# A fused two-block transformer kernel on one core: the modulation and compression weights begun by a program on GpSimd instead of ScalarE, and the engines' loops written out

## The reference

```python
def first_block(x, c, ...):            # 2 layers
    for i in range(2):
        mod = silu(c) @ ada_w[i] + ada_b[i]            # 1024 x 6144: six vectors of 1024
        sh_a, sc_a, g_a, sh_f, sc_f, g_f = split(mod, 6)
        h = rms_norm(x, attn_norm[i]) * (1 + sc_a) + sh_a
        y = sparse_mixer(...) if i == 0 else diff_mixer(...)
        x = x + g_a * y
        h = rms_norm(x, ffn_norm[i]) * (1 + sc_f) + sh_f
        x = x + g_f * swiglu(h, gate[i], up[i], down[i])
    return x

def second_block(x, c, ctx, c_ctx, ...):   # 2 layers; 6 vectors each for x and for ctx
    # layer 0: pooling mixer and squared-ReLU MLP, on x and on ctx
    # layer 1: attention of x over ctx and x, and squared-ReLU MLP, on x
    return rms_norm(x, final_g)
```

## Time and profile before

| | us |
|---|---|
| median of 3 runs | 1786.71 (1785.96 to 1787.14) |
| span of the profiled execution | 1788.7 |
| PE busy in it | 1598.4 (89%) |
| DVE busy | 923.8 (52%) |
| ACT busy | 730.1 (41%) |
| POOL busy | 0.2 (0%) |

### The profile page before, as it was taken

One profiled execution on the slowest core, in us unless ns is written; L12 is line 12 of the kernel. 1 busy time (PEld: TensorE's weight loads), 2 busy tenths in 40 slices (PEclk: granted clock), 3 DMA queues, 4 the chain that ended last, 5 costly groups with the idle time before them and its releaser, 6 DMA issues.

```text
span 1788.7 us, 26203 instructions
## 1 busy us (share of the span) xinstructions
PE 1598.4 (89%) x10441; PEld 1347.2 (75%) x10441; DVE 923.8 (52%) x1534; ACT 730.1 (41%) x1064; POOL 0.2 (0%) x4
## 2 busy tenths in 40 slices
PE   3966998999989888999988999889999796989997
PEld 2753587899877656898767998678987673779985
DVE  2582245434566685433466445653355586354455
ACT  1431153433444433444334554344444443345543
POOL 0000000000000000000000000000000000000000
PEclk9987797999999889999998999889999897999998
DMA  9843702895545445998752645639756353536552
GB/s 354 303 136 123 249 29 71 279 306 170 185 135 173 143 163 167 308 306 301 266 191 71 187 165 190 199 101 307 251 188 204 102 183 97 165 121 188 165 190 80
DMA packets 165526, 335.94 MB, mean 188 GB/s; under 512 B 8128, under 2 KB 109128, under 8 KB 165192
## 3 DMA queue, kind: packets, MB, share of 16 engines
q1 hardware_dynamic: 134432, 226.71, 38.2%
q10 hardware_dynamic: 31016, 108.16, 18.2%
HBM read 333.79 MB, written 1.05 MB: 187 GB/s over the span
## 4 chain that ended last, share of the span: by engine, by line
PE 81%; DVE 12%; ACT 3%; DMA 2%; issue 2%; ACTq 0%; SPq 0%; DVEq 0%
PE ps L1526 21%; PE ps L1527 21%; PE ps L1528 21%; PE ps L1498 5%; PE ps L1667 2%; DVE wlo L930 2%; PE ps L1664 1%; DVE work L1015 1%; DVE res L1017 1%; PE ps L1752 1%; PE ps L1702 1%; PE ps L1735 1%; DMA ring<-in_ada_w_dram 1%; PE ps L1823 1%; PE ps L1731 1%
## 5 line engine op out<-in xcount | busy, mean ns | idle before, releaser
L930 DVE TENSOR_TENSOR wlo<-wraw,whi 128x1024 fp32r<-128x1024 f32 (+1 forms) x424 | 498.0, 1216 | 420.6 <-ACT whi L542 420.3
L542 ACT ACTIVATE whi<-wraw 128x1024 fp32r<-128x1024 f32 (+1 forms) x424 | 422.8, 1044 | 442.1 <-PE ps L1528 419.5
L1526 PE MATMUL ps<-hT_hi,whi 128*128 128x256 f32 x1472 | 422.6, 287 | 4.3 <-DVE hT_lo L1070 4.3
L1527 PE MATMUL ps<-hT_lo,whi 128*128 128x256 f32 x1472 | 417.0, 283 | 0.0
L1528 PE MATMUL ps<-hT_hi,wlo 128*128 128x256 f32 x1472 | 416.8, 283 | 0.0
L1526 PEld LDWEIGHTS ps<-hT_hi,whi 128*128 128x128 f32 x1472 | 282.4, 192 | 23.6 <-issue 23.4
L1528 PEld LDWEIGHTS ps<-hT_hi,wlo 128*128 128x128 f32 x1472 | 282.6, 192 | 0.0
L1527 PEld LDWEIGHTS ps<-hT_lo,whi 128*128 128x128 f32 x1472 | 282.5, 192 | 0.0
L1526 PE MATMUL ps<-whi,act_hi 128*128 128x512 f32 x560 | 219.3, 392 | 0.0
L1527 PE MATMUL ps<-wlo,act_hi 128*128 128x512 f32 x560 | 218.3, 390 | 0.0
L1528 PE MATMUL ps<-whi,act_lo 128*128 128x512 f32 x560 | 218.2, 390 | 0.0
(11 more groups left out here) (199 smaller groups left out, 1435.8 us busy)
## 6 DMA issues: line engine op xcount, KB each, us to landing
wraw<-in_mlp_w_dram SPq DMA_DIRECT2D x96, 1024.0 KB, 5.3
ring<-in_ada_w_dram ACTq DMA_DIRECT2D x90, 1024.0 KB, 5.2
wraw<-in_ffn_w_gate_dram SPq DMA_DIRECT2D x22, 1024.0 KB, 6.0
wraw<-in_ffn_w_up_dram SPq DMA_DIRECT2D x22, 1024.0 KB, 6.7
wraw<-in_ffn_w_down_dram SPq DMA_DIRECT2D x22, 1024.0 KB, 5.0
wraw<-in_diff_w_in_dram SPq DMA_DIRECT2D x12, 1024.0 KB, 5.0
wraw<-in_attn_w_qkv_dram SPq DMA_DIRECT2D x12, 1024.0 KB, 4.9
wraw<-in_sp_w_in_dram SPq DMA_DIRECT2D x8, 1024.0 KB, 12.7
```

Source lines behind the costliest of these rows:

```text
L542: nc.scalar.activation(whi[:, u % 2, part], wraw[:, u % 4, part], ACT.Copy).then_inc(hi_ready, 1)
L930: nc.vector.tensor_tensor(wlo[:, u % 2, part], wraw[:, u % 4, part], whi[:, u % 2, part].bitcast(F32), ALU.subtract).then_inc(lo_ready, 1)
L1526: mm(dst, s_hi, m_hi, start=start, stop=False, skip_group_check=skip)
L1527: mm(dst, s_hi, m_lo, start=False, stop=False, skip_group_check=skip)
```

## The change

All ring transfers are begun by a program of POOL that does nothing else. It runs through the units in order; the waits in `ring_dma` are the same. ACT's calls of `ring_fill`, `ada_step` and `ada_body_unit` are gone, with nothing in their place. A compression unit is now begun as two transfers of half the size, and PE waits for both. ACT keeps the bias transfers and those of the pooling matrices.

```diff
-        def ring_dma(eng, r, k=None):
+        def ring_dma(eng, r):
...
             if r >= EARLY.stop:
                 before = r - 1 - (len(EARLY) if r < EARLY.stop + 2 else 0)
-                eng.wait_ge(ring_used, before if k is None else k * 4 + before)
+                eng.wait_ge(ring_used, before)
...
                 dst = dst.rearrange("p (k e) -> p k e", k=8)
                 src = w1c[a][:, b * 8:(b + 1) * 8, :]
+                eng.dma_start(dst[:, 0:4, :], src[:, 0:4, :]).then_inc(sem("cmp_half"), 16)
+                dst, src = dst[:, 4:8, :], src[:, 4:8, :]
             eng.dma_start(dst, src).then_inc(early_full[r] if r in EARLY else ring_full[r % 2], 16)
...
+            if ring_unit(r)[0] == "cmp":
+                eng.wait_ge(sem("cmp_half"), 16 * (r - CMP_AT + 1))
...
-            ring_fill(1)
-            act.wait_ge(sem("small_params"), 128)
-            ring_fill(8)
             act.wait_ge(sem("modrow_zero"), 1)
             bias(0)
             act.wait_ge(sem("paramT_ready"), 1)
...
             norm_rows()
-            ada_step(8)
             split_unit(0)
...
             c0 = CMP_AT
-            ring_fill(c0 + 4)
             act.wait_ge(ring_used, c0 + 4)
...
             ins.then_inc(sem("cmp_silu"), 1)
-            ring_fill(c0 + 6)
-            ada_step(4)
             act.wait_ge(sem("cmp_shift"), 1)
             nc.scalar.activation(cmp_s, cmp_s, ACT.Exp, scale=float(HD) ** -0.5).then_inc(sem("cmp_exp"), 1)
-            ada_step(4)
...
+        @block.gpsimd
+        def _(pool):
+            ring_dma(pool, 0)
+            pool.wait_ge(sem("small_params"), 128)
+            for r in range(1, RING_UNITS):
+                ring_dma(pool, r)
```

The second part concerns the loops. In SP, ACT, DVE and PE each `Fori` over bodies of four units becomes a Python loop that writes out every unit, with constants instead of registers in waits and addresses. The order of the units is kept. On PE:

```diff
-                n = bodies(s_)
-                for first, many, ada in loops_of(name):
-                    if ada:
-                        bank7_wait()
-                    with pe.Fori(first, first + many) as k4:
-                        for j in range(4):
-                            hidden_unit(s_, j, k4)
-                            if ada:
-                                vector_unit(LOOP_PLAN[name][0], j, k4)
-                for i in range(4 * n, s_["count"]):
+                first, many = STREAM_PLAN.get(name, (0, 0))
+                for i in range(s_["count"]):
                     hidden_unit(s_, i)
+                    if i < 4 * many:
+                        vector_unit(first + i // 4, i % 4)
```

More of the change, by code:

```diff
@@ L504, in link @@
                 act.wait_ge(chain, chained[0])
[L506 to L521, removed]
             def bias(l):
@@ L574, in stream @@
                     act.wait_ge(hid_done, hid_base[name[4:]] + s_["count"])
-                n = bodies(s_)
-                for first, many, ada in loops_of(name):
-                    if ada and many == 1:
-                        for j in range(4):
-                            if s_["kind"] != "down":
-                                hidden_out(s_, j)
-                            split_unit(s_["base"] + j + 2)
-                            ring_fill(ring_at(LOOP_PLAN[name][0], j) + 3)
-                        continue
-                    with act.Fori(first, first + many) as k4:
-                        for j in range(4):
-                            split_weights(s_, j + 2, k4)
-                            if s_["kind"] != "down":
-                                hidden_out(s_, j, k4)
-                            if ada:
-                                ada_body_unit(name, j, k4)
-                    if ada:
-                        ring_next[0] += 4 * many
-                for i in range(4 * n, s_["count"]):
+                for i in range(s_["count"]):
+                    if i < s_["count"] - 2:
+                        split_unit(s_["base"] + i + 2)
                     if s_["kind"] != "down":
                         hidden_out(s_, i)
-                    if not (hold_last and i == s_["count"] - 1):
+                    if i == s_["count"] - 2 or i == s_["count"] - 1 and not hold_last:
                         split_unit(s_["base"] + i + 2)
@@ L811, in _ @@
             out_turn(1)
-            row_segment("out1", ada=True)
+            row_segment("out1")
             next_panel()
@@ L1621, in down_segment, with unit @@
                     mm(ps[:, D_BANKS[q], :], zero16[0:1, 0:P], zero16[0:1, :], start=True, stop=False, skip_group_check=True)
-                def unit(i, k4=None):
+                def unit(i):
                     u = s_["base"] + i
-                    last = k4 is None and i == s_["count"] - 1
+                    last = i == s_["count"] - 1
                     for kk, t in TILE_LAST if last else PAIR_LAST:
                         if t == 0:
-                            unit_wait(u, kk, k4)
+                            unit_wait(u, kk)
                         for h in range(2):
@@ L1636, in unit @@
                     ins.then_inc(unit_done, 1)
-                n = bodies(s_)
-                for first, many, ada in loops_of(name):
-                    if ada:
-                        for j in range(4):
-                            unit(j)
-                            vector_unit(LOOP_PLAN[name][0], j)
-                        continue
-                    with pe.Fori(first, first + many) as k4:
-                        for j in range(4):
-                            unit(j, k4)
-                for i in range(4 * n, s_["count"]):
+                first, many = STREAM_PLAN.get(name, (0, 0))
+                for i in range(s_["count"]):
                     unit(i)
+                    if i < 4 * many:
+                        vector_unit(first + i // 4, i % 4)
             def norm():
```

172 lines of the change are left out of this document (67 added, 105 removed).

## The result

| | before | after |
|---|---|---|
| median of 9 runs | 1787.14 us (1785.96 to 1791.89) | 1799.05 us (1793.69 to 1809.5) |
| profiled execution: time, span | span 1788.7 us | 1806.62, span 1804.8 us |
| granted clock of PE, mean | 0.934 | 0.928 |

The ratio is 1.0072, 95% interval [1.0048, 1.0095]: slower, by 0.7%. Forecast were 1785.0 us and a range up to 1795. The times of the changed kernel form two groups: five between 1793.7 and 1799.0 us, and four between 1805.0 and 1809.5 us. Its profiled execution is one of the upper group, and a part of its 16 us belongs to that group alone, as will be seen. The two groups differ in TensorE's clock: its mean over the run is 0.927 or 0.928 in the four upper ones and 0.933 to 0.936 in the five lower ones.

A forecast was written before the change was run, and what follows sets the result against it. The prediction took PE, busy 89% of the span, as the bound, with only its waits to win. Start -3.0 and compression stage +1.3 gave -1.7, taking the median 1786.71 to 1785.0 us; range 1778 to 1795.

The forecast's parts named there:

- The start, -3.0: Kernel start: ACT, freed of ring issues, begins the squares at about 14.2 instead of 17.20, gaining 3.0 us.
- the term for the tile's landing: Kernel start: the first weight tile still takes 9.09 us, sharing the bus with two ring transfers as before.
- A modulation unit by POOL, extra 1.0: Ring: from freed slot to landed data, a modulation unit begun by POOL takes 1.0 us more than by ACT.
- A compression unit by POOL, extra 2.0: Compression stage: a compression unit begun by POOL in two halves takes 2.0 us more than by ACT.
- the fourth lands later too, but behind 5.1 us of PE's work: Compression stage: 5.1 us of PE's work covers the fourth compression unit's later landing; PE is through at 170.9, not 168.9.
- +1.3 at its end: Compression stage: with extras of 1.0 and 2.0, the seventh modulation unit lands at about 201.3 against 199.97, costing 1.3 us.
- 1.0 extra is just hidden: Second attention: slack of 0.6 and some 0.3 us hides 1.0 us extra; beyond it each us costs one, once.
- The loops, 0: Written-out loops on all engines: PE has nothing to win, and fetching the longer program is costed at 0.
- stalls of a longer program: Whole kernel: stalls from the longer written-out program, given 0.04 of the chance of being slower by over 0.2%.
- the fourth rival: Kernel start: the earlier norm meets a full bus and gains nothing; only +1.3 is left, 1788 us; chance 0.12.
- the slow one: POOL's transfers take 2 to 3.5 us more each, compression waits grow; 1792 to about 1797 us; chance 0.27.
- The rival of the clock: Compression stage: PE's clock stays at 2.4 GHz and the stage ends some 6 us earlier; -9, 1778 us; chance 0.11.

The follow-up runs named there:

- e2: The kernel before with all loops of the four engines written out, ring still begun by ACT; 1786.5 us, ratio 0.9973.
- e12: The changed kernel, unaltered, profiled once more in a single run; 1793.65 us.
- e7: The changed kernel plus 52 filler products on PE in the pause near 600 us, ahead of the second attention; 1792.38 us, ratio 1.0011.
- e3: The changed kernel with the four compression units begun undivided by ACT, modulation units still by POOL; 1786.22 us, ratio 0.997.
- e4: The changed kernel with dynamic_dma_scratch_size 2048 instead of 1024 and a semaphore per compression unit for its halves; 1786.48 us, ratio 0.9986.
- e8: e3 plus 52 filler products on PE in the pause near 600 us, ahead of the second attention; 1781.58 us, ratio 0.9951.

## Why the prediction was wrong

- **What bounds the kernel**: right. The streams are PE's alone, and what moved lies at the start, in the compression stage and in the clock.
- **The start, -3.0**: the order of the steps was right and the size was not. The squares came 2.1 us earlier, the forecast had 3.0; the term for the tile's landing (9.09 kept) measured 9.90. Of seven profiles with ACT's ring the mean drift at 50 us is 0.0, of seven with POOL's -1.2: the start is worth about 1.2 us. The profiles with ACT's ring alone spread from -1.5 to +1.1, so a single one can't tell it, and by an estimate from that spread the gain is uncertain by some 0.4 us.
- **A modulation unit by POOL, extra 1.0**: right. In the chain above a freed slot (186.29) is followed by 0.44 until POOL begins and 5.85 to the landing, together 6.29, against 5.32; at 199.13 it is 0.30 + 5.58 against 5.18. That is 0.7 to 1.0. The landing alone gives 0.3 to 0.5 of it (median 5.7 against 5.2, or 5.4 with ACT's ring in e2), and the 0.3 to 0.44 until POOL begins come on top.
- **A compression unit by POOL, extra 2.0, and "the fourth lands later too, but behind 5.1 us of PE's work"**: this is the step that failed. I priced each transfer by itself and took it that two halves would be on their way together, as with ACT. The runs showed that with this setting POOL doesn't begin a half before the last one has landed: four halves take 18.5 us from the first issue (153.98) to the last landing (172.47). PE starts the third unit at 163.09, 1.0 later than forecast, but the fourth at 172.60, where the forecast's steps have it at 167.2. PE is through with the units at 177.9 instead of the 170.9 of my steps. The line with `dynamic_dma_scratch_size=1024` stood in the kernel's setup, and the trace of before had no transfer begun by POOL (its page lists no software queue) that could have shown its effect.
- **The rest of the compression stage, "+1.3 at its end"**: measured +6.4 and +4.7 in the two profiles against the first of before. PE's waits for the ring were forecast at about 4, 3, 1 to 2, 1 and 3 us, 12 to 13 in all; they came to 19.7, of which 10.4 at the compression units, where 4 had been forecast. Part of the 9 us comes back, since POOL begins the first modulation unit at 168.69, as early as ACT did, and it lands while PE is still with the compression units.
- **The second attention**: "1.0 extra is just hidden", right: PE doesn't wait for the ring there. Its clock was no step of my sum. I had the clock only as a gain of one stage; that a stretch of 24 us in another could come at half the clock (0.50), for 12 us, was in none of the rivals, and it makes the upper group and a part of the median.
- **The loops, 0**: right for the streams, to 0.01 us; the 2 to 4 us of the medians are open, as said above. The chances held 0.04 for stalls of a longer program and a little of the fourth rival. The profiles show no such stall, neither a place nor a price of one: PE's idle time with no releaser is 5.0 and 0.6 us in e2, as in the kernel before.
- **The rivals**: the slow one (0.27) has the sign and about the time (1792 to 1797), but by a mechanism that isn't the one found. It priced a slower transfer of every kind, deciding from 1.4 us of extra. The extra of the common kind stayed at 1.0, and it was only the order of the halves. Its top of about 1797 was near the lower group (median 1795.5); the range ended at 1795 and so missed the median of all nine runs, 1799.05. The rival of the clock (0.11) came out in part only: from 182 to 197 us the clock was 0.66 instead of 0.50, with PE idle for 3 us of the 15, and the stage ended later all the same.

In sum: the halves cost 9 to 11 us (by the drift of the compression stage, +5.7 in the mean of after, e12 and e7 and -3.2 in the mean of e3, e4 and e8, of which e7 has +6.0 and e8 -4.1; by the medians of e7 and e8, 10.8). The start gives about 1.2, and the modulation units by POOL together with it no difference that e2 and e3 can tell (0.3 us). The profiles put the rest at places where the clock changes.

## What to carry to other kernels

Before transfers are moved to GpSimd, look at how many of them must be on their way at once, and at `dynamic_dma_scratch_size` in the program's setup: here two halves of a unit began 0.75 us apart with 2048 and 4.6 to 4.7 us apart with 1024. The sign in this trace is a DMA issue on POOL that begins when the last one has landed (4.4 us), with idle time before it (3.9 us) that has no releaser. And when two profiles differ, subtract the starts of the same instructions first: it shows at once which stage moved, and a second profile of the same kernel tells which of these steps are the clock's.

## What the hardware showed unexpectedly

- With `dynamic_dma_scratch_size=1024` three modulation transfers of 1 MB were begun in a row, but of the halves of 512 KB written as rows of 1 KB only one at a time; with 2048 at least seven of the one and three of the other. A half moved as 128 packets of 4 KB, where ACT's queue moved 1 KB packets.
- PE ran 24 us at half the clock (0.50) while busy throughout (23.90 of 23.90 us), after a pause of 0.8 us that the same kernel had in another execution too (e12), with the clock at 1.00 on both sides. That alone is 12 us of 1800.
- With 52 small products in a pause of 7 us the median was 4.6 us lower (e8 1781.58 against e3 1786.22, on two chips whose runs of before differ by 1.0), though at the place itself the profiles show 1.1 us.
